# A decoder trunk's expert stage with narrow and wide steps alternating from its fourth step to its last, and the routing arithmetic on VectorE

## The reference

```python
def moe_swiglu(h, router_w, w_gu, w_down):          # xf: 256 tokens x 1024
    logits = (xf @ router_w).astype(jnp.float32)
    top_v, top_i = lax.top_k(logits, 2)
    gates = jax.nn.softmax(top_v, axis=-1)
    cw = jnp.sum(jax.nn.one_hot(top_i, 8) * gates[..., None], axis=1)
    for e in range(8):
        out = out + cw[:, e:e + 1] * swiglu(xf, w_gu[e], w_down[e])
    # swiglu(h) = (silu(h @ W_gate) * (h @ W_up)) @ W_down, 1024 -> 3584 -> 1024
```

## Time and profile before

| | |
|---|---|
| device time, three runs | 1645.05, 1645.96 (median), 1647.24 us |
| profiled execution: its own time | 1646.65 us |
| its span, first to last instruction | 1644.9 us |
| TensorE busy | 1610.6 us, 98% |
| VectorE busy | 1321.9 us, 80% |
| ScalarE busy | 1105.0 us, 67% |
| GpSimd busy | 227.9 us, 14% |
| expert stage, from its first gather matmul | 753.0 us to the end |

### The profile page before, as it was taken

How to read it: one execution, slowest core, us unless ns; L and a number is a source line. 1 busy time by engine, 2 the same in 40 slices (tenths; PEclk the granted TensorE clock), 3 DMA queues, 4 the chain that set the end, 5 groups by cost and what they waited for, 6 DMA issues and landing times.

```text
span 1644.9 us, 22857 instructions
## 1 busy us (share of the span) xinstructions
PE 1610.6 (98%) x8096; PEld 1347.2 (82%) x8096; DVE 1321.9 (80%) x1121; ACT 1105.0 (67%) x1069; POOL 227.9 (14%) x402
## 2 busy tenths in 40 slices
PE   9999999999999999999999999999999999999996
PEld 7988888888889888888888888778888878878875
DVE  6567756544566577568998999999999999999998
ACT  5355744444344566537776888877888788888885
POOL 0034440000000444406940000000000000000000
PEclk9999999999999999999999999999999999999998
DMA  8744454555545444545999999999999999999995
GB/s 337 275 171 163 167 180 159 211 192 190 181 177 179 177 156 164 186 176 215 404 366 362 371 422 422 422 386 362 419 422 421 423 350 404 422 421 421 375 416 209
DMA packets 71771, 488.44 MB, mean 297 GB/s; under 512 B 8651, under 2 KB 11932, under 8 KB 13212
## 3 DMA queue, kind: packets, MB, share of 16 engines
q1 hardware_dynamic: 68908, 483.37, 74.7%
q10 hardware_dynamic: 2800, 4.23, 0.7%
HBM read 484.94 MB, written 2.62 MB: 296 GB/s over the span
## 4 chain that ended last, share of the span: by engine, by line
PE 71%; DVE 10%; DMA 8%; issue 7%; ACT 3%; DVEq 0%; ACTq 0%; SPq 0%
PE bank L430 16%; PE bank L432 16%; PE bank L431 16%; DMA w_raw<-expert_slabs 8%; DVE w_lo L426 4%; PE bank L2135 3%; PE bank L2136 3%; PE bank L1895 3%; PE bank L1897 3%; PE bank L1898 3%; DVE e_uy L426 2%; ACT w_hi L417 1%; DVE e_v L423 1%; PE bank L2101 1%; DVE X L1605 1%
## 5 line engine op out<-in xcount | busy, mean ns | idle before, releaser
L426 DVE TENSOR_TENSOR w_lo<-w_raw,w_hi 128x2048 fp32r<-128x2048 f32 x288 | 655.9, 2298 | 206.9 <-ACT w_hi L417 205.7
L417 ACT ACTIVATE w_hi<-w_raw 128x2048 fp32r<-128x2048 f32 x288 | 550.3, 1919 | 382.1 <-PE bank L432 265.7
L430 PE MATMUL bank<-w_hi,hT 128*128 128x512 f32 x708 | 280.9, 397 | 1.9 <-DVE w_lo L1285 1.9
L432 PE MATMUL bank<-w_hi,hT 128*128 128x512 f32 x708 | 276.9, 391 | 0.0
L431 PE MATMUL bank<-w_lo,hT 128*128 128x512 f32 x708 | 276.3, 390 | 0.0
L430 PEld LDWEIGHTS bank<-w_hi,hT 128*128 128x128 f32 x708 | 133.4, 188 | 28.2 <-issue 2.1
L432 PEld LDWEIGHTS bank<-w_hi,hT 128*128 128x128 f32 x708 | 133.2, 188 | 28.3
L431 PEld LDWEIGHTS bank<-w_lo,hT 128*128 128x128 f32 x708 | 133.5, 189 | 26.3
L432 PE MATMUL bank<-w_hi,cT_lo 128*128 128x512 f32 x352 | 137.3, 390 | 0.0
L426 DVE TENSOR_TENSOR e_uy<-w_raw,e_k 128x2048 fp32r<-128x2048 f32 x56 | 128.3, 2291 | 9.4 <-ACT e_k L417 9.3
L430 PE MATMUL bank<-w_hi,cT_hi 128*128 128x512 f32 x336 | 131.4, 391 | 0.0
(11 more groups left out here) (375 smaller groups left out, 3043.0 us busy)
## 6 DMA issues: line engine op xcount, KB each, us to landing
w_raw<-expert_slabs SPq DMA_DIRECT2D x334, 1024.0 KB, 8.9
w_raw<-mix_slabs SPq DMA_DIRECT2D x88, 1024.0 KB, 4.8
w_raw<-dense_slabs SPq DMA_DIRECT2D x33, 1024.0 KB, 4.7
bias_lines<-bias ACTq DMA_DIRECT2D x1, 1536.0 KB, 7.5
X<-in_x SPq DMA_DIRECT2D x2, 512.0 KB, 5.8
bias<-bias_lines SPq DMA_DIRECT2D x1, 1024.0 KB, 6.9
yT<-in_ffn_norm_g ACTq DMA_DIRECT2D x2, 512.0 KB, 5.3
v_buf<-expert_slabs SPq DMA_DIRECT2D x1, 1024.0 KB, 4.7
```

The lines of the kernel that those rows point to most:

```text
L417: act.activation(hi_slot(n), raw_of(n, early), ACT.Copy).then_inc(hi_ready, 1)
L426: eng.tensor_tensor(lo_slot(n), raw_of(n, early), hi_slot(n), ALU.subtract).then_inc(lo_ready, 1)
L430: pe.matmul(dst, hi, whi, start=first, stop=False, skip_group_check=True)
L432: return pe.matmul(dst, lo, whi, start=False, stop=last, skip_group_check=True)
```

## The change

The order of work in the expert stage is new on all five engines. Three wide steps stand alone; from then on a narrow and a wide step alternate, so that the narrow expert is always three steps behind: it begins when its wide partner is at step 3, and ends when the next wide one has done three. Three narrow steps are left for the end, with the last down rows. A loop body is seven such *pairs* (i = 0 to 6, 84 halves); four of them (i = 3 to 6) also stand ahead of the loop. The wide output is put out in pair 1, the narrow one in pairs 3 and 4, the gathers stand in pairs 6, 0 and 2, the seats' spreads in pairs 2 and 5. `fold_turn` is gone. The routing chain runs on VectorE between the splits of the opening steps, in 38 operations. Core of the diff (the helpers keep their work, and take step numbers instead of block numbers):

```diff
+LEAD = 3
+BODY_STEP = LEAD + 2 * (MSTEPS - LEAD)
+BODY_HALF = 6 * BODY_STEP - 4
         @block.gpsimd
-            pool.wait_ge(places_out, 1)
-            chain(pool.tensor_copy(key[:, :], places[:, 2, :]))
...
-            pool.tensor_copy(ctl_i[:, :], ctl[:, :]).then_inc(route_ready, 1)
         @block.vector
+            def name_experts():
...
+                chain(dve.tensor_tensor(terms[:, 0, :, :], src[:, 0, :].unsqueeze(1).to_broadcast([P, COLS, 2 * EXPERTS]),
+                                        col_no[:, :, :], ALU.mult))
+                chain(dve.tensor_reduce(ctl[:, 1:1 + COLS], terms[:, 0, :, :], AX, ALU.add))
+                dve.tensor_copy(ctl_i[:, :], ctl[:, :]).then_inc(route_ready, 1)
+            def seat_columns(r):
+                shape = [P, 2, COLS, 2 * EXPERTS]
+                chain(dve.tensor_tensor(terms[:, :, :, :], src[:, r + 1:r + 3, :].unsqueeze(2).to_broadcast(shape),
+                                        col_no[:, :, :].unsqueeze(1).to_broadcast(shape), ALU.mult))
+                chain(dve.tensor_reduce(seats[:, r:r + 2, 1:COLS], terms[:, :, 1:COLS, :], AX, ALU.add))
+                def pair_of_steps(i, j, n, cyc):
...
+                    after = i == LEAD + 1 and not opening
+                    if after:
+                        add_narrow(j, 0)
+                    lo(cyc, n + 6)
+                    if after:
+                        add_narrow(j, 1)
+                    if i == 1:
+                        take_y(2 * j + 1, 4)
+                    lo(cyc, n + 7)
+                    if after:
+                        add_narrow(j, 2)
+                    if i == 0:
+                        gathered(j + 1, 1, 3)
+                    turn_lo(s - 1, 0)
+                    lo(cyc, n + 8)
+                    if after:
+                        add_narrow(j, 3)
+                    lo(cyc, n + 9)
+                    if i == 2:
+                        pick_set(2 * j + 4, 2 * j + 3, False)
+                    if i == 5:
+                        pick_set(2 * j + 5, 2 * j + 4, True)
+                    lo(cyc, n + 10)
+                    summed(s, v)
+                    lo(cyc, n + 11)
+                    if i == LEAD and not opening:
+                        take_y(2 * j + 2, 6)
+                    if i == 1:
+                        keep_gates(j)
+                        add_wide(j, 0)
+                    lo(cyc, n + 12)
+                    if i == 1:
+                        add_wide(j, 1)
+                    lo(cyc, n + 13)
+                    if i == 1:
+                        add_wide(j, 2)
+                    two_lo(s, 1)
+                    lo(cyc, n + 14)
+                    if i == 2:
+                        gathered_n(j + 1)
+                    gated(s + 1, at + 10)
+                    lo(cyc, n + 15)
+                    if i == 1:
+                        add_wide(j, 3)
+                    if i == 6:
+                        gathered(j + 2, 0, 3)
+                    lo(cyc, n + 16, n + 17)
+                def opening_steps():
+                    used = MOE0
+                    gated(0, used + 4)
+                    lo(0, 6)
+                    rank_experts()
+                    lo(0, 7)
+                    file_experts()
+                    lo(0, 8)
+                    turn_lo(0, 0)
+                    name_experts()
+                    lo(0, 9, 10)
+                    gated(1, used + 8)
+                    lo(0, 11)
+                    seat_rows()
+                    seat_columns(0)
+                    lo(0, 12)
+                    turn_lo(1, 1)
+                    duo_constants()
+                    pick_set(1, 1, True)
+                    lo(0, 13)
+                    seat_columns(2)
+                    lo(0, 14)
+                    gated(2, used + 12)
+                    lo(0, 15)
+                    pick_set(2, 1, False)
+                    lo(0, 16, 17)
+                    gathered_n(0)
+                    lo(0, 18, 19)
+                    for i in range(LEAD, MSTEPS):
+                        pair_of_steps(i, -1, BODY_HALF - BODY_HALVES + 12 * i, 0)
         @block.tensor
+                def pair_of_steps(i, j, n, cyc):
...
+                    pe.wait_ge(e_silu, s)
+                    if i == LEAD:
+                        pe.wait_ge(n_act, j + 2)
+                        pe.wait_ge(n_dve, j + 2)
+                    unit(n, cyc, 0, narrow=True)
+                    if i == 0:
+                        pe.wait_ge(xg_dve, 2 * j + 3)
+                        gather(j + 1, 1, 3)
+                    if i == LEAD + 1 and not opening:
+                        scatter_narrow(j, 3)
+                    turn(s - 1)
...
+                    unit(n + 2, cyc, 1, narrow=True)
+                    add_low(v, 0)
+                    if i == LEAD + 1 and not opening:
+                        pe.wait_ge(x_add, 8 * j + 11)
+                    down(n + 4, cyc, s - 2, 1, narrow=not (opening and i == LEAD), first=i == LEAD + 1)
+                    if i == 1:
+                        scatter_wide(j, 0, 1, 2)
...
+                    unit(n + 6, cyc, 0, low=v)
+                    if i == 1:
+                        scatter_wide(j, 3)
+                    if i == 2:
+                        pe.wait_ge(spread_ready, 2 * j + 3)
+                        gather_n(j + 1)
+                    turn(s)
+                    unit(n + 8, cyc, 1)
+                    if i == 6:
+                        pe.wait_ge(spread_ready, 2 * j + 4)
+                        gather(j + 2, 0, 3)
+                    if i == 1:
+                        pe.wait_ge(x_add, 8 * j + 7)
+                    down(n + 10, cyc, s - 1, 0, first=i == 1)
+                    if i == LEAD and not opening:
+                        scatter_narrow(j, 0, 1, 2)
+                def closing_steps(j):
...
+                    add_low(v + 2, 1)
+                    pe.wait_ge(xg_dve, 2 * j + 3)
+                    scatter_wide(j, 0, 1, 2)
+                    down_half(n + 18, cyc, s + 1, 0, 0, narrow=True)
+                    turn(s + 2)
+                    scatter_wide(j, 3)
+                    down_half(n + 18, cyc, s + 1, 0, 1, narrow=True)
+                    down(n + 20, cyc, s + 2, 1, narrow=True)
+                def scatter(b, i, by, banks):
...
+                    if i == 3:
+                        pe.wait_ge(x_add, 4 * b + 1)
```

More of the change, by code:

```diff
@@ L578, in _, with gate_up, down_rows, load_all @@
-            stream_expert(0, 0, opening=True)
+            def gate_up(e, m):
+                return [one(expert_slabs, BLOCK_HALVES * e + 6 * m + i) for i in range(4)]
+            def down_rows(e, m):
+                return [one(expert_slabs, BLOCK_HALVES * e + 6 * m + 4 + i) for i in range(2)]
+            def load_all(n, halves, cyc):
+                for i, half in enumerate(halves):
+                    load_half(sp, MOE0 + n + i, half, cyc)
+            first = gate_up(0, 0) + gate_up(0, 1) + gate_up(0, 2) + down_rows(0, 0)
@@ L579, in _ @@
+            for n in range(3):
+                load_half(sp, MOE0 + n, first[n])
+            job_in_bank(sp, 1, ("values", HEADS - 1), 7)
+            load_early(sp, MOE0 + 3, first[3])
+            sp.wait_ge(biased, DEPTH * HEADS)
+            load_early(sp, MOE0 + 4, first[4])
+            for n in range(5, 14):
+                load_half(sp, MOE0 + n, first[n], slot_free=n in (9, 10))
             sp.wait_ge(route_ready, 1)
             duos = sp.value_load(ctl_i[0:1, 0:1], min_val=DUOS, max_val=DUOS + SLOTS)
[L582 to L601, removed]
@@ L717, in _ @@
-            chain(pool.tensor_scalar(src[:, 5, 0:EXPERTS], narrow[:, :], float(-NARROW), None, ALU.mult))
-            for h in range(2):
-                chain(pool.tensor_copy(src[:, 3:5, EXPERTS * h:EXPERTS * (h + 1)], gates[:, :, :]))
-            each = [P, TT, EXPERTS]
-            main, rest = src[:, 1:3, 0:EXPERTS], src[:, 1:3, EXPERTS:2 * EXPERTS]
-            chain(pool.tensor_tensor(rest, places[:, 0:2, :], cap[:, :].unsqueeze(1).to_broadcast(each), ALU.subtract))
-            chain(pool.tensor_scalar(within[:, :, :], rest, 0.0, None, ALU.is_lt))
@@ new lines, in opening_steps @@
+                def opening_steps():
+                    for hf in range(2):
+                        rows_in(0, hf)
+                        unit_half(0, 0, 0, hf)
+                    unit(2, 0, 1)
+                    pe.wait_ge(e_silu, 1)
+                    unit(4, 0, 0)
+                    turn(0)
+                    pe.wait_ge(places_out, 1)
+                    unit(6, 0, 1)
+                    spread(0, pick, 7)
+                    pe.wait_ge(e_silu, 2)
+                    unit(8, 0, 0)
+                    turn(1)
+                    unit(10, 0, 1)
+                    gather_n(0)
+                    down(12, 0, 0, 0, first=True)
+                    pe.wait_ge(shift_ready, 2)
+                    pe.wait_ge(spread_ready, 1)
```

(2 more changed lines are left out.)

995 lines of the change are left out of this document (345 added, 650 removed).

## The result

The changed kernel takes 1662.5 us (median of 4 runs, 1659.1 to 1663.9) against 1645.6 of before (4 runs beside them): a ratio of 1.0098, interval 1.0081 to 1.0116. That is 17 us slower, where 1643 was forecast, and outside the range of 1627 to 1656. The profiled execution has a span of 1662.2 us.

The account below looks back on a forecast made before the run. VectorE, TensorE and transfers were taken as within 1.3 us of each other per pair. Opening 811.4 + 118.7, bodies 3 x 215.5, closing 50.8 + 14.8 gave a 1642.2 us span, so 1643 us; range 1627 to 1656.

Parts of the forecast that it names:

- Opening: Before the loop: VectorE's work, with an 11 us routing chain, lets the first pair begin at 811.4, the loop at 930.1.
- TensorE's own work of a body: Loop body of seven pairs: 200.2 us plus 11.3 of border work on TensorE, 211.5 us.
- Pair 1: In each body, TensorE waits 1.6 us at the fourth wide scatter for VectorE's first addition; the pair takes 32.0 us.
- Pair 4: In each body, the fourth narrow scatter waits 1.0 us and the down behind it 0.9, both for additions; 31.0 us.
- a body was taken to cost the same however it is looped: Loop: all three bodies were summed at the same 215.5 us each.
- third rival: Opening worse: dearer chain, longer TensorE stand, or a longer loop body fed late; 1649 to 1653 us, chance 0.16.
- Closing: After the loop: last matmul starts 50.8 us later, with TensorE waits of 1.3, 2.0 and 1.1 us for summed products.
- the dealt-out work adds up: Bodies: TensorE's and VectorE's extra work each stretch their own pairs; 219 us a body, 1654 us, chance 0.17.
- my 215.5: Loop body: forecast us for its seven pairs together, against 217.2 before.

Follow-up runs that it names:

- all_four: Changed kernel with three bodies written out on four engines, fourth wide scatter later, third wide addition earlier, pair 4's narrow scatter and addition reordered, opening's narrow rows early: 1640.4 us.
- fourth_and_third: Changed kernel with pair 1's fourth wide scatter behind the second wide unit and the third wide addition one split earlier on VectorE: 1653.1 us.
- written_out: Changed kernel with the loop of three bodies written out on TensorE, VectorE, ScalarE and SyncE: 1655.9 us.
- tensor_alone: Changed kernel with the three bodies written out on TensorE only, the other engines keeping the jump back: 1663.9 us.
- before_long: Kernel before the change, its inner loop over four pairs of steps written out on TensorE, VectorE and ScalarE, order untouched: 1656.6 us, against 1645.6.
- narrow_rows_early: Changed kernel with VectorE taking the lo part of the narrow rows in the opening as soon as half 14 is split: 1662.9 us.
- columns_twice: Changed kernel with the opening's four VectorE operations that seat rows in columns done twice: 1666.5 us.

## Why the prediction was wrong

By its own terms the sum was off by 20 us of span: 1642.2 forecast, 1662.2 measured.

- **Opening, right.** 811.4 against 810.8, chain 11 against 10.8. VectorE's sum set this time, as forecast; that TensorE lost its 11 us in four waits and at half clock made no difference. The loop began at 931.5 on TensorE instead of 930.1: 1.4. A second stretch at half clock, from 812.3 to 815.6, costs 1.7 and was not in the forecast.
- **TensorE's own work of a body, mis-sized.** I counted 211.5. It is 213.0, the first body's 217.9 less its waits of 2.9, 1.1 and 0.9 from start to start; `all_four` has 214.1 in each of three bodies, with 0.9 of waiting, or 213.2. The old body's 217.2 thus held 4 us of waits, and not the 6 that I meant to win; between 1142.0 and 1359.2 the trace of before lists 3.6. Three times 1.5 is 4.5 us. Part of it is that the second matmul behind a wait comes 0.33 us after the first and not 0.23.
- **Pair 1, mechanism right, size wrong.** Forecast 1.6, measured 2.7, and the matmul behind starts 0.2 later still. I had TensorE reach the scatter 1.7 us after the product's end; it was 0.4 (1202.0 against 1201.56). From there to the end of the addition VectorE took 3.2 us, as counted (3.1). With 1.3 a body it makes 3.9 us. `fourth_and_third` shows that the whole wait was avoidable.
- **Pair 4, right.** 1.0 and 0.9 forecast, 0.96 and 0.72 measured.
- **The step that failed: a body was taken to cost the same however it is looped.** Bodies 2 and 3 take 4.9 and 5.8 us more than body 1. TensorE's stands are 2.4 each from start to start over the usual spacing, a late product behind one of them 0.7, and the rest, 1.8 and 3.4, is time at 1.2 GHz: one stretch behind a stand and two behind the scatter's wait. Together 10.7 us, of which the jump made some 7.2. The other 3.4 belong to a second term that I had put at nothing without a reason: TensorE's clock, which my sum held at one level through every wait. I had the jump as half a sentence of the third rival, "a longer loop body is fed late", priced only with the rest of that rival (1649 to 1653) and looked for at the loop's start, not at its jumps; `written_out`, `tensor_alone` and `before_long` show it. The diff itself said where to look: TensorE's loops over steps had gone, and the body had grown from 604 rows to 1020.
- **Closing, right.** 51.5 against 50.8, waits of 1.0, 2.1 and 0.5 against 1.3, 2.0 and 1.1; 0.7.

1.4 + 4.5 + 3.9 + 10.7 + 0.7 is 21.2. The 1.2 too many are, but for 0.1 a body, the 0.5 that my 215.5 held beyond 211.5 and 3.5 of waits.

The rival "the dealt-out work adds up" gave 219 a body and 1654. The first body's 217.9 comes near it, but not for its reason: TensorE's extra and VectorE's did not stretch one another; the order put one particular addition too late. With the two orders mended the dealt-out work is hidden as the change meant, and the body is 3 us shorter than before's.

## What to carry to other kernels

Before unrolling inner loops into a longer outer body, count its instructions on every engine, and look for waits charged to "issue" at the old jumps: a stand that was absent on TensorE at 604 rows was there at 1020, VectorE and SyncE had their own, and taking it from TensorE alone won nothing. When a wait is moved out of the way, look at once at the next user of the same buffer, for the wait may be handed on to it, and move its releaser too. A gap of over 2 us on TensorE was followed in some cases by 3.4 us at half clock, which costs 1.7 more.

## What the hardware showed

- **The jump back over a long body.** TensorE stood 2.2 us (1020 rows in the body) and 3.1 us (1016 rows, `before_long`), not at 604; VectorE 3.3 to 3.6 at 260 rows, not at 169, and not visibly at 257 (`before_long`); SyncE loaded nothing for about 4 us at 263 rows. Rows are counted in the written order of the program. Straight code of three times the length showed no stand. The Trainium skill (Runtime: NRT & Kernel Launch, "Instruction fetch mechanics") says that fetching runs ahead in sequence only, and that a taken branch to a target outside the pages held forces a fetch before the engine goes on. The traces agree as to the jump. It gives 512 instructions held for most engines, and VectorE's body of 260 rows stood all the same. By which length a jump becomes dear was not measured, nor whether length alone decides it or also where the target lies in the code.
- **The clock after a stand.** Behind equal stands of 2.2 us the clock stayed at 2.4 GHz once (at 1151.78) and fell to 1.2 GHz once, for some 3 us (at 1374.56). In `narrow_rows_early`, whose bodies are the same, it fell behind both, and behind the first body's scatter too (0.51 from 982.3 to 985.7). I can't say what decides it.
- **What stays open.** ScalarE's own stand could not be told from its waits for TensorE. `columns_twice` cost 4.0 us and not the 2.9 that its first pair was late; 1.1 is within the spread of the runs of both. In its trace low clock falls elsewhere than in the changed kernel's: from 986.0 to 989.4 it was granted 0.50, where the other has 1.00, so the two sums cannot be compared to the microsecond.
